# Three gaps of 16 words in SBUF: the weights' low parts and hidden_lo start at 0 modulo 128 bytes instead of 64

## What is computed

```python
def swiglu(h, w_gate, w_up, w_down):                 # first model
    return (jax.nn.silu(h @ w_gate) * (h @ w_up)) @ w_down

for e in range(N_EXPERTS):                           # 8 experts, D_FF_EXPERT = 3584
    y_e = swiglu(t, w_gate[e], w_up[e], w_down[e]).astype(jnp.float32)
    out = out + gates[:, e:e + 1] * y_e

x = x + 0.5 * swiglu_ffn(h, ffn1_w_gate[l], ffn1_w_up[l], ffn1_w_down[l])   # second model
...                                                  # mixer, with w_in and w_out
x = x + 0.5 * swiglu_ffn(h, ffn2_w_gate[l], ffn2_w_up[l], ffn2_w_down[l])
```

## The kernel before

| tensor | before | with the change |
|---|---|---|
| weights_hi0 to 2 | 64 | 64 |
| weights_lo0 to 2 | 64 | 0 |
| x_parts (dense tokens, last hidden rows) | 64 | 64 |
| hidden_hi | 64 | 64 |
| hidden_lo | 64 | 0 |
| x_pair (experts' gathered tokens) | 0 | 0 |
| mix_parts, mixer's low parts (c_low), consts, mslot0 to 2 | 0 | 0 |
| mslot3 and its parts, xn, xT, scratch | 64 | 64 |
| c.mixT (second mixer's rows, fp32) | 64 | 0 |

## Time and profile before

### The profile page before, as it was taken

The page is one execution under the profiler, slowest core; times in us unless marked ns, Lnnn a source line. Parts: engine busy times, 40 slices in busy tenths (PEclk is TensorE's granted clock), DMA queues, the critical chain, the costliest instruction groups (busy, mean ns, idle before and its releaser), DMA issues.

```text
span 2403.7 us, 34175 instructions
## 1 busy us (share of the span) xinstructions
PE 2382.4 (99%) x12542; PEld 2017.0 (84%) x12542; DVE 1872.4 (78%) x1961; ACT 1438.0 (60%) x1474; POOL 14.2 (1%) x34
## 2 busy tenths in 40 slices
PE   8999999999999999999999999999999999999998
PEld 7788899888888888888888888888788888897887
DVE  7767786678888888888888898677966676688666
ACT  6645455567777777777777776555254454544444
POOL 1000000000000000000000010000000000000000
PEclk9999999999999999999999999999999999999999
DMA  8375143459999999999999996853355566533653
GB/s 301 116 251 177 68 147 130 146 207 376 380 377 348 374 379 378 348 377 377 377 348 373 381 395 246 278 177 123 132 193 175 194 227 230 176 126 123 200 191 125
DMA packets 315952, 603.73 MB, mean 251 GB/s; under 512 B 9120, under 2 KB 135200, under 8 KB 315552
## 3 DMA queue, kind: packets, MB, share of 16 engines
q1 hardware_dynamic: 314160, 592.70, 69.1%
q10 hardware_dynamic: 1136, 7.87, 0.8%
q0 software_dynamic: 576, 2.10, 0.2%
HBM read 597.91 MB, written 8.91 MB: 252 GB/s over the span
## 4 chain that ended last, share of the span: by engine, by line
PE 94%; DVE 2%; ACT 1%; DMA 1%; DVEq 1%; issue 0%; SPq 0%; ACTq 0%
PE bank L205 20%; PE bank L206 20%; PE bank L207 19%; PE bank L1218 17%; PE bank L1222 9%; PE bank L3513 1%; PE bank L2955 1%; PE bank L3440 1%; PE bank L2230 1%; PE bank L2240 1%; DMA mslot<-in_e_w_in 1%; PE bank L2930 1%; PE bank L1714 1%; PE bank L1058 0%; PE bank L2149 0%; PE bank L2249 0%
## 5 line engine op out<-in xcount | busy, mean ns | idle before, releaser
L3205 DVE TENSOR_TENSOR weights_lo<-mslot,weights_hi 128x2048 fp32r<-128x2048 f32 x336 | 767.5, 2291 | 117.5 <-ACT weights_hi L3098 116.5
L3098 ACT ACTIVATE weights_hi<-mslot 128x2048 fp32r<-128x2048 f32 x336 | 644.0, 1919 | 217.4 <-PE bank L207 214.2
L1370 DVE TENSOR_TENSOR weights_lo<-scratch,weights_hi 128x2048 fp32r<-128x2048 f32 x165 | 377.2, 2289 | 166.3 <-ACT weights_hi L1363 166.2
L1218 PE MATMUL bank<-x_parts,weights_hi 128*128 128x512 f32 x1760 | 441.2, 392 | 1.8 <-DVE x_parts L921 1.8
L1218 PEld LDWEIGHTS bank<-x_parts,weights_hi 128*128 128x128 f32 x1760 | 319.4, 189 | 63.8 <-DVE x_parts L921 2.4
L205 PE MATMUL bank<-weights_hi,x_pair 128*128 128x512 f32 x896 | 356.9, 398 | 0.2 <-issue 0.2
L206 PE MATMUL bank<-weights_lo,x_pair 128*128 128x512 f32 x896 | 351.4, 392 | 0.0
L207 PE MATMUL bank<-weights_hi,x_pair 128*128 128x512 f32 x896 | 349.9, 391 | 0.0
L1363 ACT ACTIVATE weights_hi<-scratch 128x2048 fp32r<-128x2048 f32 x165 | 315.3, 1914 | 49.3 <-PE bank L207 49.0
L205 PE MATMUL bank<-weights_hi,hidden_hi 128*128 128x512 f32 x808 | 315.9, 391 | 0.0
L206 PE MATMUL bank<-weights_lo,hidden_hi 128*128 128x512 f32 x808 | 315.2, 390 | 0.0
(11 more groups left out here) (561 smaller groups left out, 2735.0 us busy)
## 6 DMA issues: line engine op xcount, KB each, us to landing
mslot<-in_o_moe_w_gate SPq DMA_DIRECT2D x112, 1024.0 KB, 6.8
mslot<-in_o_moe_w_up SPq DMA_DIRECT2D x112, 1024.0 KB, 6.8
mslot<-in_o_moe_w_down SPq DMA_DIRECT2D x112, 1024.0 KB, 6.9
scratch<-in_ffn_w_gate SPq DMA_DIRECT2D x44, 1024.0 KB, 5.2
scratch<-in_ffn_w_up SPq DMA_DIRECT2D x44, 1024.0 KB, 5.1
scratch<-in_ffn_w_down SPq DMA_DIRECT2D x44, 1024.0 KB, 5.0
mslot<-in_o_w_in SPq DMA_DIRECT2D x7, 2048.0 KB, 10.8
scratch<-in_e_ffn_w_gate SPq DMA_DIRECT2D x11, 1024.0 KB, 5.2
```

What stands on the lines that cost most here:

```text
L1218: pe.matmul(m.ps[bank + j][:, :], hi[:, k, cols(j)], both, start=(k == 0), stop=False)
L1370: dve.tensor_tensor(m.wlo[to][:, :], m.fslot[i], m.whi[to][:, :], ALU.subtract).then_inc(m.sig["f_lo"], 1)
L3098: act.activation(m.whi[(place + half) % PLACES][:, :], r.slot[slot + half], ACT.Copy).then_inc(s["r_hi"], 1)
L3205: dve.tensor_tensor(m.wlo[i][:, :], r.slot[slot + half], m.whi[i][:, :], ALU.subtract).then_inc(s["r_lo"], 1)
```

## The change

Three tensors of 16 words (64 bytes) are put in: before weights_lo0, before x_parts and between hidden_hi and hidden_lo. What overlays these through `scratch` moves along with them: the delta-net's buffers from offset 14336 on by 32 words, and c.mixT by 16 words. The last tensors before x_pair are made 48 words shorter, and x_pair stays where it was. The delta-net's buffers keep their residue. No instruction, semaphore or transfer is added, taken out or moved: on each of the five engines the two programs have the same rows in the same order.

```diff
+PHASE = 16
...
     m.whi = [sb(f"weights_hi{i}", PIECE, F32R) for i in range(3)]
+    sb("phase0", PHASE)
     m.wlo = [sb(f"weights_lo{i}", PIECE, F32R) for i in range(3)]
+    sb("phase1", PHASE)
     m.x2 = cut(sb("x_parts", KT * 2 * SEQ, F32R), 0, KT, 2, SEQ)
     m.xh, m.xl = m.x2[:, :, 0, :], m.x2[:, :, 1, :]
-    m.hh, m.hl = sb("hidden_hi", HALF, F32R), sb("hidden_lo", HALF, F32R)
-    with nc.sbuf_tensor("mixer_lows", [P, f0 + 3 * PIECE - 6 * PIECE - KT * 2 * SEQ - 2 * HALF], F32R) as lows:
-        m.c_low = [cut(lows, f0 - 6 * PIECE - KT * 2 * SEQ - 2 * HALF + i * KT * DC, KT, DC) for i in range(2)]
-    sb("scratch_rest", f0 + PIECE - 6 * PIECE - KT * 2 * SEQ - 2 * HALF)
+    m.hh = sb("hidden_hi", HALF, F32R)
+    sb("phase2", PHASE)
+    m.hl = sb("hidden_lo", HALF, F32R)
+    free = f0 - 6 * PIECE - KT * 2 * SEQ - 2 * HALF - 3 * PHASE
+    with nc.sbuf_tensor("mixer_lows", [P, free + 3 * PIECE], F32R) as lows:
+        m.c_low = [cut(lows, free + i * KT * DC, KT, DC) for i in range(2)]
+    sb("scratch_rest", free + PIECE)
     m.xg = cut(sb("x_pair", 2 * PIECE, F32R), 0, 2, KT, 2 * P)
...
-    o.dec, o.LT, o.T, o.TT, o.BV = pair(6144), pair(8192), pair(10240), pair(12288), pair(16384)
+    o.dec, o.LT, o.T, o.TT, o.BV = pair(6144), pair(8192), pair(10240), pair(12288), pair(16384 + 2 * PHASE)
...
-    c.mixT = m.scr(10240, KT, SEQ)
+    c.mixT = m.scr(10240 + PHASE, KT, SEQ)
```

More of the change, by code:

```diff
@@ L2013, in odd_mem @@
     pair = lambda at: [m.scr(at + t * 1024, GH, P) for t in range(NT)]
-    o.dec, o.LT, o.T, o.TT, o.BV = pair(6144), pair(8192), pair(10240), pair(12288), pair(16384)
+    o.dec, o.LT, o.T, o.TT, o.BV = pair(6144), pair(8192), pair(10240), pair(12288), pair(16384 + 2 * PHASE)
     o.AT, o.U = o.dec, o.LT
-    o.Y = [m.scr(14336 + a * 512, 4, P) for a in range(2 * NT)]
-    o.S, o.tmp = pair(14336)
-    o.KD = m.scr(18432, GH, P)
+    o.Y = [m.scr(14336 + 2 * PHASE + a * 512, 4, P) for a in range(2 * NT)]
+    o.S, o.tmp = pair(14336 + 2 * PHASE)
+    o.KD = m.scr(18432 + 2 * PHASE, GH, P)
     o.gb = [o.KD, o.T[0]]
-    o.qdT = m.scr(19456, GH, P)
+    o.qdT = m.scr(19456 + 2 * PHASE, GH, P)
     first = SMALL_COLS["w_a"][0]
-    o.sg = [m.scr(20480, D), m.small[:, first:first + D]]
+    o.sg = [m.scr(20480 + 2 * PHASE, D), m.small[:, first:first + D]]
     o.o = m.scr(2048, NT, GH, P)
-    o.sq = m.scr(21504, GH, SEQ)
+    o.sq = m.scr(21504 + 2 * PHASE, GH, SEQ)
     o.xh, o.xl = m.odd_x2[:, :, 0, :], m.odd_x2[:, :, 1, :]
```

## The result

The change makes the kernel slower: 2424.53 us median of 5 runs (2424.11 to 2425.57) against 2406.08 (2405.57 to 2406.63) for the kernel before, ratio 1.0077, 95% interval 1.0066 to 1.0088. The forecast was 2400.0 with a range of 2389 to 2413. The profiled execution spans 2423.4 us, 19.7 more than before, at the same granted clock (0.999); it was the longest of the five, and by the medians the change costs 18.5 us.

A forecast was written before the change was run, and what follows sets the result against it. TensorE was taken as the bound, through the distance between matmul starts. Terms -9.5 + 0 + 1.2 + 3.8 - 0.8 - 0.5 = -5.8 us, off the 2405.79 us median, gave 2400.0 us, range 2389 to 2413.

The forecast's parts named there:

- What bounds the kernel: Whole kernel: TensorE busy 99%, no wait paces it; time is matmul count times the distance between starts.
- same side: Moving and stationary starts equal modulo 128 bytes; claimed best for 512 columns, 226.7 ns a matmul.
- other side: Moving and stationary starts 64 bytes apart modulo 128; claimed best for 256 columns, 113.3 ns a matmul.
- Step 1: Dense FFN low products of 256 columns (narrow): blocks of eight fall from 0.950 us by 0.043, 220 times, -9.5 us.
- Step 2: FFN and expert down products: every step keeps the same side, so 0; upper bound 12.1 us slower.
- moving against the next stationary: Down products: a matmul's moving operand collides with the next one's stationary operand, whose load runs beside it; cost 0.
- Step 3: Down products on the last hidden rows in x_parts: weights_lo at 0 makes the pattern mixed, +1.2 us.
- Step 4: Experts' gate and up: other, same, other side gives 230.3 ns a matmul, +3.8 us; bounds -5.9 to +7.5.
- fully mixed case: Experts' gate and up at the mixed pattern's 231.7 ns: three steps take 0.695 us, +7.5 us.
- Step 5: Mixer products on weights_lo up to -0.8 us, second mixer's output product -0.5 us.
- Step 6: DVE and ACT writing the moved tensors: side makes nothing and PE waits for neither, 0.
- down is disturbed as well: Rival, down products: own operands or side changes cost up to 12.1 us, 2412 us (2415.8 with gate and up); chance 0.3.

The follow-up runs named there:

- e4: Kernel before with only a 32-word gap in front of x_parts, moving x_parts, hidden_hi and hidden_lo 128 bytes against the weights; 2425.65 us.
- e8: Kernel before with other gaps: weights at 64, x_parts and hidden at 0, x_pair at 192 modulo 256 bytes; 2417.51 us.
- e13: Kernel before with other gaps: weights_hi at 64, weights_lo at 192, x_parts, hidden and x_pair at 128 modulo 256 bytes; 2414.83 us.
- e6: Kernel before with other gaps: weights_lo alone at 128, weights_hi, x_parts, hidden and x_pair at 64 modulo 256 bytes; 2422.66 us.
- e12: Kernel before with other gaps: weights_lo, hidden_lo and x_pair at 128, weights_hi, x_parts and hidden_hi at 64 modulo 256 bytes; 2424.22 us.
- e3: Kernel before with x_pair moved 16 words, from 0 to 64; router's tables overlapped, so output wrong, stands for time only; 2402.31 us.
- e14: Kernel before with other gaps: weights_lo alone at 0, weights_hi, x_parts, hidden and x_pair at 64 modulo 256 bytes; 2409.19 us.
- e2: Kernel before with only the 16-word gap in front of hidden_lo, weights_lo left at 64; 2414.69 us.
- e5: Kernel before with x_pair at 64 and a 64-word gap before x_parts, so x_parts and hidden lie 256 bytes further from the weights; 2402.36 us.
- e10: Kernel before with other gaps: weights at 64, x_parts and hidden at 96, x_pair at 32 modulo 256 bytes; 2434.39 us.
- e11: Kernel before with other gaps: weights at 64, x_parts and hidden at 160, x_pair at 224 modulo 256 bytes; 2441.61 us.

## Why the prediction was wrong

**What bounds the kernel** held: no new wait, clock and DVE unchanged (2290 ns for 2291), and the whole change of time lies in the distances of matmul starts. So did "an address can only count by changing that distance".

**The rule failed, and with it all that rests on it.** "I call an operand's start modulo 128 bytes its side" was read off the kernel before, in which the matrices compared lie 0 or 64 bytes apart modulo 256, one way or the other. There "same side" is always distance 0. But "other side" is distance +64 at 512 columns (weights at 64 on x_pair at 0) and -64 at 256 (x_parts at 64 on mix_parts at 128). Modulo 128 bytes the sign is lost and so is the distance 128, and no part of the prediction asked for the period. The three gaps added up to 128 bytes in front of x_parts; e4 has that displacement alone and costs 19.5 us.

- *Step 1, narrow, -9.5.* Measured -3.7. The 113.3 ns were taken from a mixer product at distance -64, and the change gave narrow +64. It turned the mixer product itself to +64 as well, and that went from 0.1 to 4.4 ns over the grid; narrow took 3.6, and only 57 of 220 blocks reached 0.91 us. At -64 narrow does what the step asked for, 1.3 and 1.5 us over the grid in e8 and e13, but not behind wide ones at 0 (7.05 in e6). Overlooked beside it: wide, which the step left "where it is", lost its lock (+4.8), because x_parts against weights_hi went from 0 to 128. The step had bounds of 0 and a gain, and none for a loss.
- *Step 2, down, 0.* Measured +10.7, near its upper bound of 12.1. This is the step that turned the sign. By "moving against the next stationary every step keeps the same side"; e12 gives that pairing distance 0 and finds 4.1 ns over the grid. In the change the distances were further off: 128 for weights_hi on hidden_hi, -64 for weights_lo on it, +64 for weights_hi on hidden_lo.
- *Step 3, last hidden rows, +1.2.* Measured +1.2 (all three lines together); the size was right, the reason was not: the distance of weights_hi to x_parts became 128 as well.
- *Step 4, gate and up, +3.8.* Measured +5.2, within its bounds; three steps take 0.693 us where 0.691 was forecast and 0.695 was the fully mixed case.
- *Step 5, mixers, -1.3.* Measured +1.7 over all other products, of it 1.6 in the mixers' products of x_parts on mix_parts and on low parts, whose distances changed sign (276 to 280 ns). The second mixer's output product did speed up, all at distance 0 now, by about 0.2 us of the 0.5.
- *Step 6, DVE and ACT, 0.* Held.

Of the rivals, "down is disturbed as well" had the mechanism nearest to the truth and a chance of 0.3, at 2412 to 2415.8. What lifts it to 2424.5 is in the main the wide products (+4.8), the 5.8 us of narrow that didn't come, and the mixers (3.0 worse than forecast).

The Trainium skill, "TensorE: Matmul & The Clock Gate", Part 2, gives moving operand and weight load independent read ports, by which no placement would count. The runs don't agree with that conclusion: the same instructions took 2400.8 to 2441.6 us, with nothing but starts moved. What in the reading of operands collides, no run shows. In e3 only the stationary operand of gate and up was moved, and the product went from 228.9 to 226.7 ns.

**Left open.** Whether a matmul's own pair, the pair with its neighbour's load, or the sequence of several steps decides: e12 speaks against the neighbour alone (down) and against the own pair alone (gate and up). With one step of three off, e14 (-64) takes 2.4 ns a matmul, near the mean of its steady rows, (0.7 + 0.7 + 6.6) / 3 = 2.7; e2 (-64, by the stationary operand) takes 4.3, and e6 (+64) 5.3, where the mean would be 1.5. And no run had own distances all 0 with the neighbours' not. Why +64 and -64 differ, and why their order turns round between 512 and 256 columns, was measured and not explained. The writes of other engines are no likely cause: down matmuls with VectorE idle and ScalarE busy beside them take 0.5 ns over the grid in the kernel before and 5.2 in the changed one, with VectorE busy 0.9 to 1.1 and 5.4 to 5.5, so the layout makes its difference either way.

## What to carry to other kernels

When matmul streams run back to back, look at the distance between the starts of moving and stationary operand modulo 256 bytes, and measure all four values before choosing: here 0 was best at 512 columns (up to 6.8 ns more on 226.7 for each matmul elsewhere; only wide, which stands behind narrow, did as well at +64), -64 at 256. Note distances with their sign, and compare steps that stand in one series: a mixture can cost more than any of its parts. Before inserting a gap, list every pair of tensors whose distance it changes, not just the tensor that it is meant for: here the first two gaps shifted x_parts and hidden by 128 bytes together. And a rule read from one layout holds for the differences that this layout has; where it doesn't contain the new one, the range must hold a loss for every product that reads a moved tensor.

## What the runs showed of the hardware

- The pace of fp32r matmuls with a load beside each depends on the operands' distance modulo 256 bytes, at a granted clock of 1.00: 226.7 ns to about 233.5 for 512 columns, 113.3 to about 120 for 256, with starts at multiples of 64 bytes and one distance throughout. 256 bytes more between them change nothing (e5), 128 cost 19.5 us (e4).
- Distances of 32 and 96 bytes to either side, with one start off the multiples of 64 bytes (e10, e11), make 512 columns 6.5 to 7.2 ns slower than the grid; the kernel is 28 and 35 us slower.
- In a series whose distances differ from step to step the cost isn't the mean of the steady ones: -64, 0, -64 takes 7.8 ns over the grid (e12, gate and up), where steady rows give 6.8 and 0.7.
- A block's time depends on what stood in front of it: narrow at distance -64 takes 0.7 ns over the grid behind wide ones at +64 or -64, and 4.0 (7.05 us over 1748) behind wide ones at 0.
